# Conditioning in column strips, an earlier second mixer, channel sums on VectorE and an earlier split in the last block of a fused streaming encoder layer

## The reference

```python
mod = jax.nn.silu(c) @ w_ada + b_ada                  # 9 conditioning rows -> 6 x 1024
sh1, sc1, gt1, sh2, sc2, gt2 = split(mod, 6)
h = _rmsnorm(x, g_pre_mix) * (1 + sc1) + sh1
proj = h @ w_in                                       # 1024 -> 2176
ya = pooling over windows 2/4/8/16, minus the token, per-group linear, scaled
u = a * sigmoid(g);  z = depthwise_causal(u, 31 taps) + b_dw
yb = silu((z - mean(z)) * rsqrt(var(z) + EPS) * ln_g + ln_b)     # over 384 channels
yc = b * depthwise_causal(c * h, 3 taps)
x = x + gt1 * _rmsnorm(concat(ya, yb, yc) @ w_out, g_post_mix)
h = _rmsnorm(x, g_pre_ffn) * (1 + sc2) + sh2
x = x + gt2 * _rmsnorm((silu(h @ w_gate) * (h @ w_up)) @ w_down, g_post_ffn)
```

## Time and profile before

| | us |
|---|---|
| median of 3 runs (2365.51 to 2370.28) | 2366.36 |
| profiled execution | 2368.96 |
| its span, first to last instruction | 2367.2 |
| granted TensorE clock, mean share of full speed | 0.991 |
| busy: TensorE, weight loads, VectorE, ScalarE, GpSimd | 2318.4, 2094.2, 1340.9, 1029.7, 40.2 |
| DMA: moved, mean | 361.64 MB, 153 GB/s |

### The profile page before, as it was taken

How to read it: one execution, slowest core, us unless ns; L and a number is a source line. 1 busy time by engine, 2 the same in 40 slices (tenths; PEclk the granted TensorE clock), 3 DMA queues, 4 the chain that set the end, 5 groups by cost and what they waited for, 6 DMA issues and landing times.

```text
span 2367.2 us, 30248 instructions
## 1 busy us (share of the span) xinstructions
PE 2318.4 (98%) x12452; PEld 2094.2 (88%) x12452; DVE 1340.9 (57%) x1917; ACT 1029.7 (43%) x1433; POOL 40.2 (2%) x82
## 2 busy tenths in 40 slices
PE   8999998999999999999999999999999998999998
PEld 2848897897999898899999899989889996899987
DVE  1775796569744367844357773436784433443343
ACT  2435554545353444435353435444443424433232
POOL 0000000000000000000000000000000000000000
PEclk9999999999999999999999999999999999999999
DMA  8664463344533353353344344335334432534332
GB/s 303 229 214 153 144 228 131 132 173 173 174 143 126 124 178 129 139 186 123 127 137 166 125 175 146 125 125 178 125 125 176 120 130 100 178 134 170 131 127 89
DMA packets 101743, 361.64 MB, mean 153 GB/s; under 512 B 12259, under 2 KB 14435, under 8 KB 101604
## 3 DMA queue, kind: packets, MB, share of 16 engines
q1 hardware_dynamic: 101606, 359.70, 43.3%
HBM read 340.73 MB, written 18.93 MB: 152 GB/s over the span
## 4 chain that ended last, share of the span: by engine, by line
PE 93%; DVE 4%; DMA 2%; ACT 1%; issue 1%; SPq 0%; POOL 0%; POOLq 0%; DVEq 0%; ACTq 0%
PE ps L474 92%; DVE wlo L1083 1%; PE ps L516 1%; DVE pr L1210 1%; DMA raw<-in_w_ada 1%; DMA raw<-in_w_gu 0%; DVE g_lo L1132 0%; DMA gate<-in_gpost 0%; DMA raw<-in_w_mix 0%; DVE h_lo L1125 0%; DVE xr L1156 0%; ACT whi L726 0%; ACT junk L768 0%; ACT junk L745 0%; DVE xt L1146 0%
## 5 line engine op out<-in xcount | busy, mean ns | idle before, releaser
L474 PE MATMUL ps<-h_hi,whi 128*128 128x384 f32 (+1 forms) x2928 | 958.5, 327 | 4.0 <-DVE wlo L1083 3.6
L474 PE MATMUL ps<-h_hi,wlo 128*128 128x384 f32 (+1 forms) x2928 | 954.2, 326 | 0.0
L474 PE MATMUL ps<-h_lo,whi 128*128 128x384 f32 (+1 forms) x2928 | 954.1, 326 | 0.0
L1083 DVE TENSOR_TENSOR wlo<-raw,whi 128x1024 fp32r<-128x1024 f32 x546 | 664.3, 1222 | 502.2 <-ACT whi L726 491.1
L726 ACT ACTIVATE whi<-raw 128x1024 fp32r<-128x1024 f32 x546 | 576.0, 1057 | 789.9 <-DMA raw<-in_w_gu 531.4
L474 PEld LDWEIGHTS ps<-h_hi,whi 128*128 128x128 f32 x2928 | 552.7, 189 | 10.5 <-issue 6.4
L474 PEld LDWEIGHTS ps<-h_lo,whi 128*128 128x128 f32 x2928 | 552.6, 189 | 1.9 <-issue 0.3
L474 PEld LDWEIGHTS ps<-h_hi,wlo 128*128 128x128 f32 x2928 | 552.4, 189 | 0.0
L1210 DVE SCALAR_TENSOR_TENSOR pr<-u,col,pr 128x384 f32<-128x384 f32 x450 | 260.2, 614 | 1.2
L474 PE MATMUL ps<-whi,g_hi 128*128 128x512 f32 x748 | 236.1, 397 | 12.0 <-DVE g_lo L1132 10.4
L474 PE MATMUL ps<-whi,g_lo 128*128 128x512 f32 x748 | 231.4, 390 | 0.0
(11 more groups left out here) (110 smaller groups left out, 1160.8 us busy)
## 6 DMA issues: line engine op xcount, KB each, us to landing
raw<-in_w_gu SPq DMA_DIRECT2D x264, 512.0 KB, 3.2
raw<-in_w_mix SPq DMA_DIRECT2D x150, 512.0 KB, 3.3
raw<-in_w_dn SPq DMA_DIRECT2D x132, 512.0 KB, 3.2
raw<-in_w_ada SPq DMA_DIRECT2D x48, 512.0 KB, 4.3
xt<-in_x_all SPq DMA_DIRECT2D x17, 512.0 KB, 6.2
xr<-in_x_all SPq DMA_DIRECT2D x17, 512.0 KB, 5.8
xr<-x_all SPq DMA_DIRECT2D x17, 512.0 KB, 6.0
x_all<-xr SPq DMA_DIRECT2D x5, 1536.0 KB, 7.3
```

What stands on the lines that cost most here:

```text
L474: return nc.tensor.matmul(out, lhsT, rhs, start=start, stop=stop, skip_group_check=True)
L1083: tt(wlo[:, s, :], raw[:, s, :], whi[:, s, :].bitcast(F32), ALU.subtract).then_inc(w_lo, 1)
```

## The change

**Conditioning in strips.** `ada_units(q)` takes four units at once. Each of them has a strip of 32 PSUM partitions and of the array's columns for itself (`tile_position=(0, strip)`): first the left halves of all four, then the right halves, and only with a unit's right half is its slot given back. The four partial sums stay apart in `mod` (105 rows and the bias row instead of 9 and one). They are added when they are used: `ada_columns` is now an fp32 product with a matrix of zeros and ones, and the selecting matrices of `gate_rows` hold a one in each strip. All 24 first units come ahead of the input projection; the sixth group stands behind the eight chunks. The transposes of the second 24 come in pairs. The wait for the post-norm gains moves on VectorE from ahead of the first mixer to ahead of the first gate.

**Second block's mixer.** It starts behind the first block's low halves: five steps ahead of `normalise(0)`, two with each output unit, four instead of three with each projected unit (none beside the residual), five instead of six in each pass. The taps add up in `early`; only the last tap writes `pr` and waits for the output projection. `IN_ADA` goes from 3 to 4.

**Channel sums.** For the blocks from the second on VectorE adds the three groups (`sum_z`, `sum_squares`, two additions each), and TensorE does one product with the ones instead of three.

**Last block.** The third hidden row is split with the last output units, ahead of the residual; the squares of the residual's rows on ScalarE come one unit earlier.

```diff
-            def ada_unit(i):
-                n, g, k = UNIT["ada", i], i // KD, i % KD
...
-                pe.wait_ge(w_landed[n % RING], landed(n))
                 for h in range(2):
-                    w = slice(512 * h, 512 * h + 512)
-                    last = mm(ps[0:C_PAD, 2 + 2 * pair + h, :], c_s[:, k, :], raw[:, n % RING, w], k == 0, k == KD - 1)
-                last.then_inc(w_used, 1)
+                    for i in range(STRIPS):
+                        n, strip = UNIT["ada", STRIPS * q + i], C_PAD * i
+                        if h == 0:
+                            pe.wait_ge(w_landed[n % RING], landed(n))
+                        last = nc.tensor.matmul(ps[strip:strip + C_PAD, 2 + 2 * ADA_PAIR[g] + h, :], c_s[:, k0 + i, :],
+                                                raw[:, n % RING, 512 * h:512 * h + 512], start=k0 == 0,
+                                                stop=k0 + STRIPS == KD, tile_position=(0, strip), skip_group_check=True)
+                        if h:
+                            last.then_inc(w_used, 1)
...
-                        last = nc.tensor.transpose(ps[:, bank, o:o + MOD_K], mod[:, i, k * P:(k + 1) * P],
-                                                   ident[0:MOD_K, 0:MOD_K])
+                        last = mm(ps[:, bank, o:o + ROWS + 1], mod[:, i, k * P:(k + 1) * P],
+                                  con_a[0:MOD_K, E_FOLD:E_FOLD + ROWS + 1], True, True)
...
+                elif b and i == 2:
+                    pe.wait_ge(z_summed, b)
+                    last = mm(out, ones, pslot("g", 2)[:, 0:w], True, True)
+                elif b:
+                    pe.wait_ge(zsq_summed, b)
+                    last = mm(out, ones, pslot("b", 0)[:, 0:w], True, True)
...
-                if i < 5 * KD and i % 2:
-                    transposes(1, (i - ADA_HEAD) // 2)
+                if q < 10:
+                    transposes(1, 2 * (q - 6))
+                    transposes(1, 2 * (q - 6) + 1)
...
+                    elif k == TAPS - 1:
+                        z = tokens("a", j)
+                        if b == 1:
+                            dve.wait_ge(w_used, UNIT["out", 0, NMIX - 1] + 1)
...
+            mixer = mixing(1)
+            advance(mixer, 5)
             normalise(0)
...
+                    if c == 0:
+                        advance(mixer, IN_OUT)
...
-                    elif c and k >= NMIX - 2:
-                        hidden_low(c - 1, k - (NMIX - 2))
+                    elif c and k >= NMIX - G_RING:
+                        hidden_low(c - 1, k - (NMIX - G_RING))
...
-                        if k + 2 < NF:
+                        if k + 2 < NF and (k or c < NB - 1):
                             hidden_low(c - 1, k + 2)
...
                         elif m == s - 1:
                             finish(mixer)
+                            sum_z(c + 1)
...
+                        elif m == s + 2:
+                            sum_squares(c + 1)
```

More of the change, by code:

```diff
@@ L63 @@
 EARLY = 6
-STREAM = [("ada", n) for n in range(ADA_HEAD - 2)]
+STREAM = [("ada", n) for n in range(ADA_HEAD)]
 for j_ in range(NIN):
     STREAM.append(("in", 0, j_))
-    if j_ < 2:
-        STREAM.append(("ada", ADA_HEAD - 2 + j_))
 STREAM += [("ada", n) for n in range(ADA_HEAD, ADA_ALL)]
@@ L632, in _ @@
             pe.wait_ge(c_ready, 1)
-            for i in range(ADA_SHIFT):
-                ada_unit(i)
+            for q in range(ADA_SHIFT // STRIPS):
+                ada_units(q)
             pe.wait_ge(const_landed, 48)
@@ L885, in _ @@
                 h_split(0, k)
-                if k == 0:
-                    for i in range(ADA_SHIFT + 3):
+                if k == 3:
+                    for i in range(ADA_SHIFT + 5):
                         ahead("ada", i)
-                elif k == 2:
-                    for i in range(ADA_SHIFT + 3, ADA_HEAD - 2):
-                        ahead("ada", i)
+                elif k == 5:
+                    ahead("ada", ADA_SHIFT + 5)
+            ahead("ada", ADA_HEAD - 2)
+            ahead("ada", ADA_HEAD - 1)
             for j in range(NIN):
                 ahead("in", 0, j)
-                if j < 2:
-                    ahead("ada", ADA_HEAD - 2 + j)
                 evacuate(0, j)
@@ L1347, in finish, with add_three, sum_z, sum_squares @@
                     pass
+            def add_three(b, kind, into, done):
+                w = NT[b] * P
+                x0, x1, x2 = (pslot(kind, j)[:, 0:w] for j in range(NCONV))
+                after(own.step(tt(into, x0, x1, ALU.add)))
+                tt(into, into, x2, ALU.add).then_inc(done, 1)
+            def sum_z(b):
+                dve.wait_ge(z_ready, NCONV * (b + 1))
+                dve.wait_ge(evac_done, evac_count(b, NIN - 1))
+                add_three(b, "a", pslot("g", 2)[:, 0:NT[b] * P], z_summed)
+            def sum_squares(b):
+                dve.wait_ge(zsq_ready, NCONV * (b + 1))
+                add_three(b, "b", pslot("b", 0)[:, 0:NT[b] * P], zsq_summed)
             def centre(b):
@@ L1444, in _ @@
                         first, count = IN_PROJ[c + 1]
-                        if j >= first:
+                        if j >= first and j != j0 + 1:
                             advance(mixer, count)
```

118 lines of the change are left out of this document (57 added, 61 removed).

## The result

The changed kernel takes 2331.91 us (median of 4 runs, 2331.47 to 2333.89) against 2366.18 us beside it (4 runs): a ratio of 0.985, 95% interval 0.984 to 0.987. That is 34.3 us less, not 49.2: sign and range (2306 to 2342) hold, but the forecast of 2317.0 is missed by 15 us, and the time lies outside the forecast's own case, 2308 to 2328. The profiled execution is 2333.89 us long, its span 2332.1, its clock 0.987 of full speed.

What follows compares the result with a forecast made beforehand. TensorE, busy 98% of the span, was taken as the bound. Terms 18.5 + 10.3 + 12.9 + 0.7 + 7.0 = 49.4 us off the profiled span 2367.2 led, adjusted to the median, to 2317.0 us, range 2306 to 2342.

Steps and rivals of the forecast that it cites:

- sign: Whole kernel: the change was said to make it faster with chance 0.96, the same 0.01, slower 0.03.
- forecast's own case: Whole kernel: the main line of the prediction, 2308 to 2328 us, chance 0.69.
- case without overlap: Rival, conditioning: strips do not overlap, a group stays at 7.1 us, 2339.5 us in all; chance 0.14.
- bounds of 14 and 22: Conditioning: limits in us around the 18.5 us forecast to come off ahead of the first block's statistics.
- Second block's mixer: Second block, first pooling and sum: TensorE's 7.1 us wait and 3.2 us of slow clock go, 10.3 us.
- the sums: Channel sums from the second block on: four fewer products a block, 12.9 us over five blocks.
- One group of four units: Conditioning: strips overlap only between neighbouring records, 3.6 us a group; ring loading makes the period 6.0 against 7.1 us.
- all four at once: Rival, conditioning: four strips overlap fully, 2.5 us a group, loading 5.5, VectorE binds the second half; 2313 us, chance 0.08.
- First 24 units: Opening to the first gate rows: projections end near 105.5 against 111.6 us, six microseconds gained.
- 1 to 2 us of late units behind the x tiles: Input projection: allowance for late loads, added to seventeen projections of 2.87 us each.
- Second 24 units: Gate rows to first statistics: TensorE done at 145, VectorE at 146 to 147; second pooling product near 147 us.
- Last block: Last down product: a low half made ahead cuts a 10.1 us wait to some 3 us; 7 us gained, bounds 5 and 9.

Runs made afterwards that it cites:

- e12: Changed kernel with 24 extra products ahead of the seventh group, eight each on one, two and four strips, overwritten afterwards: 2340.93 us (one run).
- e9: Changed kernel without the second mixer's five steps ahead of the first normalising and two beside each first output unit, left to the mixer's end: 2345.18 us.
- e10: Changed kernel with the channel sums of z and its squares back on TensorE, three products each, no additions on VectorE: 2343.83 us.
- e6: Changed kernel with the second block's x tiles loaded behind the sixth projected unit, two bias rows and post-norm gains behind the tenth: 2328.5 us.
- e4: Changed kernel with the sixth group of four units ahead of the transposes of chunks 2 to 7 instead of behind them: 2330.1 us.
- e5: Changed kernel with ScalarE's last copy of conditioning sums two steps earlier, ahead of the third and fourth projected units' high weight halves: 2326.1 us.
- e8: Changed kernel with five repairs: slots given back unit by unit, sixth group amid the chunks, copy early, x tiles and gains late, squares late: 2311.71 us.
- e7: Changed kernel with the three squares of the last block's residual rows on ScalarE one down unit later, as before the change: 2328.12 us.
- e3: Changed kernel with each unit's left and right half following each other on its own strip, then the next unit: 2327.63 us.
- e1: Changed kernel with the conditioning exactly as before, units one after another; second mixer, sums on VectorE and last block's split stay: 2341.62 us.

## Why the prediction came out as it did

**The range held by luck.** It reached from 2306 to 2342 only to take in the case without overlap, which e12 refutes. The forecast's own case ended at 2328, and the 6.5 us that came ahead of the statistics lie outside its bounds of 14 and 22. Two waits that it did not have, 6.1 and 6.4 us, used up the room kept for another case.

**Right: the step "Second block's mixer", the sums, the sign.** 10.3 + 2.6 + 0.7 = 13.6 us were forecast up to the third block and 13.5 came. So close a hit is partly luck. Inside it two small terms cancel: the second block's summed squares are waited for 1.57 us, where 0.4 was forecast, and the mixer brought about that much more. And other profiles with the same order in this stage give 11.5 to 13.8 us. e9 shows its cause, and that "in time, by 0.25 us a pass" is right for the pooling; the sum behind it has 0.1 us left, or none. Sums: 12.9 us forecast, 12.6 by e10; no block from the third on waits for the summed squares.

**Wrong in kind, harmless in size: "One group of four units".** The second record of one strip beside the first of the next "and no more" is refuted: four strips run fourfold (e12), a warm group with all its units takes 1.9 us instead of 3.6. The rival *all four at once* named this mechanism, yet its 2313 us missed as well, since the ring sets the period: 6.5 us from 116.86 to 123.39, where 6.0 was forecast, whichever way strips overlap. The Trainium skill, "TensorE: Matmul & The Clock Gate", section Packing small matmuls, has weight loads overlap only across row groups and gives 2.38 times for three column tiles; here seven loads into four column strips share a row of 0.15 us beside running products, and the loads come four times as close on four strips as on one, two times on two.

**Mis-sized: "First 24 units".** This is the step that failed: 6.1 us were forecast up to the gate rows and 3.5 were lost, 9.6 of the 14.3 us by which the span's account fell short. Turning: 2.1 us taken, bounds 1.2 to 4, 4.19 measured. An fp32 product with a full weight load was priced at half a transposing load a record, but the loads are the bound; the row of the changed kernel's weight loads:

```profile
40.10 4.09 PEld L475 LDWEIGHTS ps<-con_a,mod 106*128 106x128 f32 x32 [0.84 <-issue]
```

That is 0.13 us each. The load step "1 to 2 us of late units behind the x tiles" is the larger one. The seventeen projections took 58.4 us (56.64 to 115.05) against 48.8 of work, 9.6 lost and 1.2 allowed for. 6.1 are the wait ahead of the third product, for an evacuation that stands on ScalarE behind the high halves of the fourth and fifth unit; 0.4 are the next wait, and near 2.2 the first 24 products at the lower clock level. I had seen that the sixth group moves behind the chunks, but only followed its 3.6 us on TensorE, not its slots: nothing can be loaded while it waits (DMA share 0.00 from 52 to 56 us), and then everything is asked for at once. Late, then, are units "behind the x tiles", as the step has it, but by 7.6 and 8.3 us from issue to landing, and ScalarE's order makes TensorE wait for them two units before it needs them. e6 and e4 try the two halves of this cause: without the foreign traffic ahead of those units 4.5 us come back, with the slots early 2.0, which is hardly outside the scatter.

**Mis-sized: "Second 24 units".** "2.8 us for ScalarE's last copy as before" became 6.39. ScalarE's order did not change, but the loads of its high halves did, because slots now come back in fours (e5). VectorE, held to be the bound, ended at 153.9 and was not what ended last; in e8 it is.

**Mis-sized: "Last block".** 7 us forecast, about 5.1 came. "A square" stands in the chain; there are three, 1.2 us each, ahead of the high half (e7). The bound of 5 just holds.

**Still open.** In the first block 1.1 us is lost between statistics and FFN (112.4 against 111.3 us); the trace shows a wait of 1.50 us at 237.10 for an evacuation, whose cause was not tried, but the stretch takes 110.2 to 113.3 us over the experiments, so it may be scatter. The 1.0 us gained at the end lies behind TensorE's last product, where nothing was changed; all experiments have it, and its cause stays open. The 2 us scatter of the opening was not traced either.

## What to carry to other kernels

When units are grouped for TensorE, follow the slots: the point at which each goes back sets when the next loads start, which engine's list stands behind those loads, and what other traffic they meet. Both long waits of the conditioning end with a short ScalarE copy out of PSUM that stands in an in-order list behind high halves of later units; e5 shows it for one, the trace alone for the other. Repairs of order, without a new idea (e8), gave 20 to 23 us of time on top of the 34 that the change gave. A chain behind a residual is to be read instruction by instruction: one "square" that is three cost more than the step had left.

## What the hardware showed unexpectedly

Column strips of 32 run beside each other in both orders tried, up to fourfold (e3, e12). And two waits of one length and the same instructions can leave different clocks. Before, TensorE waits 3.59 us at 68.24 and goes on at full speed; in e1 it waits 3.52 us at 69.09 and goes on at the lower level. The wait's end and a stretch, of before, then of e1:

```profile
68.24 0.35 PE L474 MATMUL ps<-h_hi,whi 128*128 128x256 f32 x1 [3.59 <-DVE wlo L1083]
...
70.00:74.00 4.00, 4.00 (x36) 4.00 (x35) 3.59 (x7) 3.90 (x6) 0.00 (x0) 1.00 0.39 136
```

```profile
69.09 0.55 PE L476 MATMUL ps<-h_hi,whi 128*128 128x256 f32 x1 [3.52 <-DVE wlo L1091]
...
70.00:74.00 4.00, 4.00 (x21) 4.00 (x20) 3.83 (x5) 2.47 (x3) 0.00 (x0) 0.50 0.12 42
```

36 product records against 21 in 4 us. With the 0.9 us by which it came to the wait later, this is most of the 3.3 us that e1 has lost by the gate rows. A forecast that adds or spares the cold clock behind a wait of this length can miss by 2 us either way.
